# Two-block transformer kernel: where the gate projections, spatial gating, branch products and output product stand in the second mixer

## What is computed

```python
x = x + 0.5 * swiglu(rmsnorm(x, ffn1_norm[l]), ffn1_w_gu[l], ffn1_w_down[l])
h = rmsnorm(x, mix_norm[l])
z = h @ w_in[l]
u = jax.nn.gelu(z[..., COL_U:COL_V], approximate=False)
v = jax.nn.gelu(z[..., COL_V:COL_CQ], approximate=False)
y_a = spatial_gating(u, v, sg_ln_g[l], sg_ln_b[l], sg_w[l], sg_b[l])
y_b = mla(z[..., COL_CQ:COL_CKV], z[..., COL_CKV:COL_KR], z[..., COL_KR:COL_QM], positions, ...)
y_c = memory_attention(z[..., COL_QM:COL_GATE], mem, ...)
gates = jax.nn.sigmoid(z[..., COL_GATE:] + b_gate[l]).reshape(B, S, N_BRANCH, D_MODEL)
merged = (gates[:, :, 0] * (y_a @ w_branch_a[l])
          + gates[:, :, 1] * (y_b @ w_branch_b[l])
          + gates[:, :, 2] * (y_c @ w_branch_c[l]))
x = x + merged @ w_out[l]
x = x + 0.5 * swiglu(rmsnorm(x, ffn2_norm[l]), ffn2_w_gu[l], ffn2_w_down[l])
```

## Time and profile before

| | us |
|---|---|
| median of 3 timed executions | 1194.31 (1192.31 to 1195.35) |
| the profiled execution, on the device | 1193.38 |
| its span (first to last instruction) | 1191.6 |
| TensorE busy with matmuls | 1120.4 (94%) |
| VectorE busy | 729.1 (61%) |
| ScalarE busy | 580.6 (49%) |
| GpSimd busy | 439.0 (37%) |

### The profile page before, as it was taken

The page is one execution under the profiler, slowest core; times in us unless marked ns, Lnnn a source line. Parts: engine busy times, 40 slices in busy tenths (PEclk is TensorE's granted clock), DMA queues, the critical chain, the costliest instruction groups (busy, mean ns, idle before and its releaser), DMA issues.

```text
span 1191.6 us, 21937 instructions
## 1 busy us (share of the span) xinstructions
PE 1120.4 (94%) x8532; PEld 1072.9 (90%) x8532; DVE 729.1 (61%) x1120; ACT 580.6 (49%) x1028; POOL 439.0 (37%) x236
## 2 busy tenths in 40 slices
PE   4789999899989999999999999889999999999999
PEld 3679999788889999999999998869996999999998
DVE  6455857886758953237777423754665776777631
ACT  3445545564555554444444445686552345444432
POOL 4440111311454544544444453324231345344353
PEclk8889999999989999999999999999997999999999
DMA  9546988323435555555555554335441444555553
GB/s 363 205 147 221 353 313 259 123 72 107 152 132 178 188 183 180 187 169 188 181 182 189 177 183 136 130 118 176 143 141 37 160 159 159 178 178 176 171 169 121
DMA packets 58260, 208.04 MB, mean 175 GB/s; under 512 B 6799, under 2 KB 8207, under 8 KB 58040
## 3 DMA queue, kind: packets, MB, share of 16 engines
q1 hardware_dynamic: 51784, 183.64, 46.2%
q0 software_dynamic: 6384, 23.09, 5.4%
HBM read 205.64 MB, written 1.06 MB: 173 GB/s over the span
## 4 chain that ended last, share of the span: by engine, by line
PE 73%; DVE 8%; issue 7%; ACT 6%; DMA 3%; POOL 1%; SPq 1%; DVEq 0%; ACTq 0%; POOLq 0%
PE bank L591 73%; DMA ring<-in_stream 3%; ACT rounded_rounded L1158 3%; DVE ring_rounded L1541 1%; PE bank L842 1%; POOL ring_rounded L1083 1%; DVE shared L1908 1%; DVE wide L1786 1%; ACT wide_rounded L1363 1%; DVE shared_rounded L1819 1%; ACT log_ms L1182 1%; DVE stats L1781 1%; ACT rinv L1186 0%; DVE part L1906 0%; DVE wide_rounded L1815 0%
## 5 line engine op out<-in xcount | busy, mean ns | idle before, releaser
L1083 POOL TENSOR_TENSOR ring_rounded<-ring,rounded_rounded 128x1024 fp32r<-128x1024 f32 x154 | 383.5, 2491 | 610.9 <-ACT rounded_rounded L1158 610.9
L591 PE MATMUL bank<-u_rounded,rounded_rounded 128*128 128x256 f32 x1528 | 440.6, 289 | 7.6 <-ACT u_rounded L1215 3.9
L591 PE MATMUL bank<-u_rounded,ring_rounded 128*128 128x256 f32 x1528 | 433.4, 284 | 0.0
L591 PE MATMUL bank<-u_lo_rounded,rounded_rounded 128*128 128x256 f32 x1528 | 430.0, 285 | 0.0
L1541 DVE TENSOR_TENSOR ring_rounded<-ring,rounded_rounded 128x1024 fp32r<-128x1024 f32 x172 | 267.9, 1558 | 242.6 <-ACT rounded_rounded L1158 242.1
L1158 ACT ACTIVATE rounded_rounded<-ring 128x1024 fp32r<-128x1024 f32 x326 | 337.9, 1051 | 151.9 <-PE bank L591 126.0
L591 PEld LDWEIGHTS bank<-u_rounded,rounded_rounded 128*128 128x128 f32 x1528 | 294.8, 193 | 11.7 <-issue 6.9
L591 PEld LDWEIGHTS bank<-u_rounded,ring_rounded 128*128 128x128 f32 x1528 | 294.8, 193 | 0.1
L591 PEld LDWEIGHTS bank<-u_lo_rounded,rounded_rounded 128*128 128x128 f32 x1528 | 293.4, 193 | 0.8
L591 PE MATMUL bank<-shared_rounded,rounded_rounded 128*128 128x256 f32 x992 | 258.4, 287 | 7.2 <-DVE shared L2057 3.9
L591 PE MATMUL bank<-wide_rounded,rounded_rounded 128*128 128x256 f32 x864 | 234.1, 286 | 14.5 <-POOL ring_rounded L1083 5.9
(11 more groups left out here) (270 smaller groups left out, 1155.9 us busy)
## 6 DMA issues: line engine op xcount, KB each, us to landing
ring<-in_stream SPq DMA_DIRECT2D x334, 512.0 KB, 3.4
ada_ring<-in_ada POOLq DMA_DIRECT2D x33, 512.0 KB, 5.3
wide<-in_mem_t SPq DMA_DIRECT2D x2, 512.0 KB, 6.4
shared<-in_ada POOLq DMA_DIRECT2D x2, 512.0 KB, 10.5
ada_ring<-in_ada SPq DMA_DIRECT2D x2, 512.0 KB, 14.3
x<-in_x_t SPq DMA_DIRECT2D x1, 1024.0 KB, 14.7
wide<-in_ada POOLq DMA_DIRECT2D x2, 512.0 KB, 21.9
wide<-in_ada SPq DMA_DIRECT2D x2, 512.0 KB, 21.4
```

Source lines behind the costliest of these rows:

```text
L591: return nc.tensor.matmul(out, lhs, rhs, start=start, stop=stop, skip_group_check=True)
L1083: pool.tensor_tensor(R(w), w, R(slot_round(q)), ALU.subtract).then_inc(slot_split_by_pool, 1)
```

## The change

The same matmuls are done, in another order.
- `sv` stands before `uq`, and its results are copied raw; the gelu follows later in one activation of 1024 columns.
- Gates 0 to 3 stand one by one between the head keys. ScalarE copies them raw, and applies the tanh later, in place.
- `su2` and `su3` stand after `scores(0)`; the loop starts at gate 4.
- The spatial products stand in turns 2 to 8 of the loop, one each and two in the last (`SPATIAL_AT`).
- Turn 10 has all eight `br_a` in place of gates, turn 11 all eight `br_b`. VectorE adds them up there.
- After the loop `br_c` is woven with the output product: for each k from 0 to 3 two `br_c`, then the step k of six output blocks (`MIX_EARLY`, in banks 3 to 6, two banks holding two blocks each). Then k from 4 to 7 for those six, then blocks 6 and 7 whole.

```diff
+RAW_GATES = 4
+MIX_BANKS = (3, 3, 4, 4, 5, 6)
+MIX_EARLY = len(MIX_BANKS)
+SPATIAL_AT = {2: (0,), 3: (1,), 4: (2,), 5: (3,), 6: (4,), 7: (5,), 8: (6, 7)}
...
 # TensorE
+            project_tokens(["sv0", "sv1"], KD, u_parts, 512, lambda: sum_squares("qm3", "ones"))
             for h in range(8):
                 project(f"uq{h}", 3, (latent, latent_lo), ...)
...
-            for b in range(4):
+            for b in range(RAW_GATES):
                 project(f"uk{b}", 2, kv_latent, ...)
...
+                project(f"gate{b}", KD, u_parts)
+                sum_k_squares(b)
             project_tokens(["uv0", "uv1"], 2, kv_latent, 512)
-            project_tokens(["sv0", "sv1"], KD, u_parts, 512)
-            for b in range(4):
+            for b in range(2):
                 project(f"su{b}", KD, u_parts)
...
             scores(0)
-            project("gate0", KD, u_parts)
-            project("gate1", KD, u_parts)
+            for b in range(2, 4):
+                project(f"su{b}", KD, u_parts)
...
             for i in range(12):
+                if i < 10:
+                    project(f"gate{2 * i + RAW_GATES}", KD, u_parts)
+                    project(f"gate{2 * i + RAW_GATES + 1}", KD, u_parts)
+                elif i == 10:
+                    pe.wait_ge(sg_ready, 4)
+                    for m in range(KD):
+                        project(f"br_a{m}", 4, (attn_a, attn_a_lo2))
+                else:
+                    for m in range(KD):
+                        project(f"br_b{m}", 4, (attn_b, attn_b_lo2), ...)
                 if i < 11:
-                    project(f"gate{2 * i + 2}", KD, u_parts)
-                    project(f"gate{2 * i + 3}", KD, u_parts)
                     scores(i + 1)
                 if i:
                     values(i - 1)
                 turn(i)
...
+                for n in SPATIAL_AT.get(i, ()):
+                    spatial(*divmod(n, TT))
...
+            def mix_step(m, k):
+
+                chunk = at["chunk"]
+                w_hi, w_lo = take()
+                give_back(mm(mix_out(m), w_hi, R(merged[:, k, :]), k == 0 and m not in (1, 3)), chunk)
+                mm(mix_out(m), w_hi, R(merged_lo2[:, k, :]))
+                return mm(mix_out(m), w_lo, R(merged[:, k, :]), stop=k == KD - 1)
+
             values(11)
...
+            for k in range(KD // 2):
+                for m in (2 * k, 2 * k + 1):
+                    project(f"br_c{m}", 4, (attn_c, attn_c_lo2), ...)
+                pe.wait_ge(merged_ready, KD + k + 1)
+                for m in range(MIX_EARLY):
+                    mix_step(m, k)
+            for m in range(MIX_EARLY):
+                for k in range(KD // 2, KD):
+                    if m == 0:
+                        pe.wait_ge(merged_ready, KD + k + 1)
+                    ins = mix_step(m, k)
...
+            for m in range(MIX_EARLY, KD):
+                project(f"mix2_{m}", KD, (merged, merged_lo2))
...
 # VectorE, after the loop
+            dve.wait_ge(branches_added, KD)
             for m in range(KD):
...
+                gate_branch(part[:, m % 2, :], 2 * KD + m, f"br_c{m}")
+                taken(f"br_c{m}")
+                v.tensor_tensor(merged_lo2[:, m, :], merged_lo2[:, m, :], part[:, m % 2, :], ALU.add).then_inc(merged_raw, 1)
                 if m:
                     rest_of_merged(KD + m - 1, m - 1, merged_lo2)
+                dve.wait_ge(merged_raw, KD + m + 1)
```

186 lines of the change are left out of this document (107 added, 79 removed).

## The result

| | before | after |
|---|---|---|
| median of 5 timed executions | 1194.31 (1191.95 to 1196.59) | 1184.11 (1182.56 to 1186.07) |
| the profiled execution, on the device | 1193.38 | 1182.56 |
| its span | 1191.6 | 1180.8 |

The ratio is 0.992, with a 95% interval of 0.989 to 0.995: 10.2 us faster by the medians, 10.8 by the spans. Forecast were 17.0 us and a range of 1171 to 1187. The sign and the range were right; the gain was 6.8 us short. 1184.1 lies outside the forecast case of 1172.5 to 1183 and inside the range only because that reaches towards the rival of slow branches.

A forecast was written before the change was run, and what follows sets the result against it. TensorE was taken as the bound, with only its waits and lower-clock time able to change. Gains of 23.9 us less 6.9 of new waits gave 17.0, so 1194.3 became 1177.3 us; 8-in-10 range 1171 to 1187.

The forecast's parts named there:

- forecast case: Whole kernel: the predicted gains and new waits hold, time 1172.5 to 1183 us, likeliest 1177.3; chance 60%.
- rival of slow branches: Turn 11 and weave: VectorE's adds and rests blocked by GpSimd splits, new waits 18.3 us, time 1188.7 us; chance 20%.
- What could be won: Queries and keys 9.2 us, end of loop 1.5, spatial products and what follows 6.2, branch products 7.0: 23.9 us.
- keys, gates, `su0`: Head keys: 1.5 us of waits with the gates among them, plus 0.3 us for `su0` awaiting the last keys' bank.
- loop, from `su2`, `su3`: Behind `scores(0)`: two following gates cover ScalarE's gelu, table loads and exponentials as four did; no new wait counted.
- `values(11)`: Turn 11: waits for the last transposes and ScalarE's 0.60 us copy of them, with handovers; 1.0 us.
- weave: Branch c with output product: 1.5 us wait at the first step, 1.0 for later ones; 2.5 us, range 1.5 to 7.
- lower clock: Weave: two waits near each other may bring the lower clock for a moment; 0.8 us, range 0 to 2.8.
- The wait of 2.70 us: After the output product, for GpSimd's last gathering add: unchanged, since blocks 6 and 7 end it as before.
- The last 200 us: End of the kernel: unchanged, since the number of chunks before is the same and the same slots fall to GpSimd.
- The loop loses its slack: Seven loop turns with spatial products: splits push VectorE past 1.1 us of slack, 16.8 us lost, time 1194.1; chance 4%.
- The rival of a clock that stays down: `br_c` and output product: 288 matmuls at 1.2 GHz cost 31.7 us, time 1209.0 us; chance 3%.

The follow-up runs named there:

- gates_after_keys: Changed kernel with gates 0 to 3 moved from among the head keys to a row after the values uv; 1190.7 us against 1184.1.
- su_raw: Changed kernel with the four u projections, copied raw, among the keys and gates 0 to 3 behind the scores of head 0; 1181.0 us against 1184.1.
- memo_bank: Changed kernel with the last memory head's values in a projection bank instead of the bank still holding the previous memory head; 1182.1 us against 1184.1.
- tail_dve: Changed kernel with all splits from the slots of branch b to the program's end on VectorE, none on GpSimd; 1183.1 us against 1184.1.
- no_weave: Changed kernel with all eight branch c products in a row, then all eight output blocks whole; 1182.6 us against 1184.1.
- before_f2_dve: Kernel before the change, with all splits of the last feed-forward part on VectorE, none on GpSimd; 1190.4 us against 1193.9.
- sg_block: Changed kernel with the eight spatial products in a row at the end of turn 9 instead of spread over turns; 1189.3 us against 1184.1.

## Why the prediction was right, and 7 us short

**What could be won** was 23.9 us, and it was won nearly whole. Keys and queries: from the first matmul of the stage to the first u projection, less the 11.5 us of gates that came in, the time fell by 8.9 us, against 9.2 - 1.5 - 0.3 = 7.4 forecast. No wait before the queries, none for ScalarE among the keys; instead one of 0.90 us in the second query, for a split. gates_after_keys shows that the gates among the keys bring the larger part. No run takes back `sv`, or branches a and b, by themselves: that they brought their share is read from the trace, where the waits before the first two queries and that of 1.46 us before `values(10)` are gone. The spatial products in the loop run at 2.4 GHz as foreseen.

**New waits** were put at 6.9 us. Measured to the end of the output product (978.24):

| term | forecast | measured |
|---|---|---|
| keys, gates, `su0` | 1.5 + 0.3 | 0.9 |
| loop, from `su2`, `su3` | 0 | 2.2 |
| start of turn 11 | 0.5 | 0.2 |
| `values(11)` | 1.0 | 2.1 |
| `br_c0` | 0.3 | 0 |
| weave | 2.5 | 1.4 + 2.0 + 1.4 = 4.8 |
| lower clock | 0.8 | 3.3 |
| sum | 6.9 | 13.5 |

The 3.3 us: the first 24 matmuls of `br_c` took 4.6 us in place of 2.9, and the 18 of the second step 3.75 in place of 2.2. The difference of 6.6 us is the shortfall: 17.0 - 6.6 = 10.4, and 10.3 were measured there. The closeness is partly luck, as the kernels also differed by 0.4 us before the stage.

1. *"I count nothing" for `su2`, `su3` behind `scores(0)`.* This step failed. Of TensorE's cover it was true; but ScalarE's exponentials of head 0 stand behind the gelu of `su3` in its program, and were 9.7 us behind their scores in place of 3.3; those of head 1 then came 5.7 us behind theirs in place of 2.2. I had looked at what covers ScalarE's work, not at what is queued before it. su_raw undoes it, and the 2.22 us go.
2. *`values(11)`, 1.0.* The mechanism was incomplete. The copy of the weights would have cost 0.69 us (memo_bank). The bank of the memory heads, emptied by VectorE behind eight products and adds, made it 2.07.
3. *Weave, 2.5.* The first wait, forecast at 1.5, was 1.41. The "1.0" for all later steps was the mis-sized term: 2.03 and 1.40. I added one blocked operation to a chain that "just fits"; tail_dve shows that the chain does not fit even with none blocked (1.69, 1.56, 2.59), since a product can stand behind a split that waits for ScalarE's rounding.
4. *Clock, 0.8.* Mis-sized: it fell behind two waits, for 1.7 and 1.6 us.
5. *The wait of 2.70 us "stays".* Wrong: 5.93, and the sum itself 0.9 us longer at 1.2 GHz. I looked at how the last two blocks end and not at the lag with which VectorE and ScalarE come to them. no_weave shows the lag to be the weave's.
6. *The last 200 us "stay".* Wrong by 4.6 us, the other way (198.9 from 992.7, 194.3 from 986.5). The slots fell to GpSimd as before, but the phase between the two engines was another. before_f2_dve shows that the change is not needed for that gain. Points 5 and 6 nearly cancel (202.6 against 203.0 us behind the output product), so the total came out as if both had been right.

**The signs.** Of those for "right", three came: no wait before the first queries, PEclk 1.00 in the loop, TensorE busy among the keys. The second was luck: with the same program up to there the clock fell behind the wait of the second turn in no_weave, tail_dve and memo_bank. The wait before `values(11)` was twice the 1 us named, and the output product ended at 978.2, not 971.6. Of those for "wrong", two came: PEclk 0.50 in the weave, twice for under 4 us, and an add of 2.30 us on VectorE in turn 11 (926.39), which cost TensorE only 0.23 us.

**The rivals.** "Branches stay slow" (1188.7) was nearest in kind: VectorE's chain made the waits there. The price lay between the two. "The loop loses its slack" did not happen with the spatial products; one turn lost 2.2 us for another reason. The rival of a clock that stays down fell: in the changed kernel it rose again within 4 us in the weave, and 5.2 us after TensorE took up work again behind the output product (at 989.7). And where I said that "the trace speaks for the kind of work as a second cause", sg_block contradicts me for the start of a fall: eight such products run at 1.00. Whether they keep the clock down once it has fallen stays open. The rule of the Trainium skill ("TensorE: Matmul & The Clock Gate", "HAM oscillation — how this bites in real kernels"), that gaps bring the fall, is the better reading of where it starts: every fall in these traces from the loop to the start of the last part has a wait of 1.46 us or more before it, at the spatial products of the kernel before some 6 us before it.

## What to carry to other kernels

When work is moved away from an engine's critical moment, ask of every engine what its next urgent instruction now stands behind in its own program; cover of the matmuls is only half of the answer. A wait that names a gathering add or a split is the end of a chain: the time between the last matmul and the first reader tells which engine lags. And a stage that "stays" because its instructions are the same can still change by 2% with the phase in which it is entered, so compare its length in both traces before a gain is put down to the edit.
